# A mixer and mixture-of-experts layer: the first token tile's expert places counted on their own, gathers spread over a pair's first chunks, the down bias moved one pair later

## What is computed

```python
h  = rms_norm(x, g_ffn)                       # x already holds x + mixers(x)
logits = h @ w_router + b_router              # 256 x 32
top_val, top_idx = lax.top_k(logits, 4)
gates = softmax(top_val)
# for each of the 32 experts e, over the tokens that chose it:
hu = h[tok] @ w_up[e] + b_up[e]               # 1024 -> 2048
x_glu, x_lin = split(hu);  x_glu = min(x_glu, 7);  x_lin = clip(x_lin, -7, 7)
act = x_glu * sigmoid(1.702 * x_glu) * (x_lin + 1)
y = (act @ w_down[e] + b_down[e]) * gate      # 1024 -> 1024
x = x + sum of y over the chosen experts
```

## Time and profile before

| | |
|---|---|
| median of 3 runs | 1045.23 us (1041.35 to 1045.49) |
| the profiled execution, its own time | 1047.88 us |
| its span, first to last instruction | 1045.8 us |
| PE busy | 998.6 us (95%), 4512 matmul passes |
| DVE busy, ACT busy | 202.4 us (19%), 114.6 us (11%) |
| DMA, queue of SP | 424.17 MB, 95.5% of 16 engines' span |
| chain that ended last | PE 70%, DMA 28% |
| mean granted TensorE clock | 0.990 |

### The profile page before, as it was taken

One profiled execution on the slowest core, in us unless ns is written; L12 is line 12 of the kernel. 1 busy time (PEld: TensorE's weight loads), 2 busy tenths in 40 slices (PEclk: granted clock), 3 DMA queues, 4 the chain that ended last, 5 costly groups with the idle time before them and its releaser, 6 DMA issues.

```text
span 1045.8 us, 10985 instructions
## 1 busy us (share of the span) xinstructions
PE 998.6 (95%) x4512; PEld 403.1 (39%) x4512; DVE 202.4 (19%) x485; ACT 114.6 (11%) x230; POOL 12.9 (1%) x26
## 2 busy tenths in 40 slices
PE   8999999999999999999999989999898989898997
PEld 4446563434343433333343434342423324242432
DVE  0456132112121111212121211211111211112112
ACT  2426110001010101010100000000001000000000
POOL 0200000000000000000000000000000000000000
PEclk9999989899999999999999999999999999999999
DMA  9955869989999999999999999999999999999996
GB/s 363 402 243 234 361 248 412 417 374 432 430 435 427 437 425 439 425 437 426 436 426 437 431 432 431 431 435 427 436 426 436 429 436 426 436 427 435 427 428 253
DMA packets 22462, 424.91 MB, mean 406 GB/s; under 512 B 3600, under 2 KB 4368, under 8 KB 6704
## 3 DMA queue, kind: packets, MB, share of 16 engines
q1 hardware_dynamic: 22064, 424.17, 95.5%
q10 hardware_dynamic: 384, 0.54, 0.2%
HBM read 423.65 MB, written 1.05 MB: 406 GB/s over the span
## 4 chain that ended last, share of the span: by engine, by line
PE 70%; DMA 28%; another core or an unknown queue 1%; ACT 1%; issue 0%; DVE 0%; SPq 0%
PE psum L1386 30%; DMA everything<-in_w_moe 27%; PE psum L1416 15%; PE psum L1072 4%; PE psum L1281 4%; PE psum L1313 3%; PE psum L1196 3%; PE psum L1039 3%; PE psum L1271 2%; PE psum L1047 2%; PE psum L1064 1%; PE psum L1055 1%; ACT everything L688 1%; PE psum L1322 0%; PE psum L1235 0%
## 5 line engine op out<-in xcount | busy, mean ns | idle before, releaser
L1386 PE MATMUL psum<-everything 128*64 128x512 f32 x2048 | 456.9, 596 | 5.3 <-DMA everything<-in_w_moe 5.1
L1416 PE MATMUL psum<-everything 128*64 128x512 f32 x1024 | 229.7, 601 | 31.8 <-DMA everything<-in_w_moe 24.3
L1386 PEld LDWEIGHTS psum<-everything 128*64 128x64 f32 x2048 | 139.7, 137 | 293.0 <-issue 283.3
L1416 PEld LDWEIGHTS psum<-everything 128*64 128x64 f32 x1024 | 76.1, 138 | 173.6 <-issue 158.3
L1004 DVE TENSOR_SCALAR everything<-psum 128x512 f32<-128x512 f32 x32 | 22.2, 692 | 408.1 <-PE psum L1386 408.1
L721 DVE TENSOR_TENSOR everything<-psum,everything 128x512 f32<-128x512 f32 (+1 forms) x38 | 25.0, 663 | 287.0 <-PE psum L1281 284.1
L1281 PEld LDWEIGHTS psum<-everything 128*128 128x128 f32 x512 | 61.7, 200 | 13.6 <-issue 13.6
L1281 PE MATMUL psum<-everything 128*128 128x128 f32 x512 | 64.7, 286 | 0.0
L679 ACT ACTIVATE everything<-everything 128x512 f32<-128x512 f32 x32 | 20.2, 630 | 380.1 <-DVE everything L1004 380.1
L1313 PE MATMUL psum<-everything 128*128 128x512 f32 x128 | 57.7, 593 | 0.0
L1072 PE MATMUL psum<-everything 128*128 128x512 f32 x96 | 42.1, 594 | 0.0
(11 more groups left out here) (160 smaller groups left out, 299.9 us busy)
## 6 DMA issues: line engine op xcount, KB each, us to landing
everything<-in_w_moe SPq DMA_DIRECT2D x81, 4096.0 KB, 44.6
everything<-in_w_moe SPq DMA_DIRECT2D x25, 2048.0 KB, 17.3
everything<-in_w_moe SPq DMA_DIRECT2D x8, 1024.0 KB, 8.5
everything<-in_w_in SPq DMA_DIRECT2D x3, 2048.0 KB, 26.7
everything<-in_w_out SPq DMA_DIRECT2D x2, 2048.0 KB, 11.7
everything<-in_w_mem_kv SPq DMA_DIRECT2D x1, 2048.0 KB, 17.8
everything<-in_w_moe SPq DMA_DIRECT2D x4, 512.0 KB, 36.0
everything<-in_w_in SPq DMA_DIRECT2D x1, 1024.0 KB, 9.4
```

What stands on the lines that cost most here:

```text
L1386: mm = pe.matmul(psum[r:r + SLOTS, bank], XT[:, k, r:r + SLOTS], weights[i][:, column:column + N], start=k == 0 and not first, stop=k == K ...
L1416: mm = pe.matmul(psum[r:r + SLOTS, DOWN_BANKS[n]], actT[:, 2 * i + k, r:r + SLOTS], slot[:, column:column + N], start=i == 0 and k == 0, s ...
```

## The change

- The placing is done tile by tile. `count(t)` on PE writes tile t's counts beside its router logits, `place_and_select(t)` on DVE makes `spots` and `sel` of that tile. The count of tile 0 stands inside the last part of `mix`, and two router steps of tile 1 ahead of `turn_h2(3)`. `gather_first(0, ...)` gathers tile 0's half of the first four pieces before the count of tile 1, `gather_first(1, ...)` adds tile 1's. All `keep_warm` matmuls are gone. Two of the four up biases of pair 0 move into the pair, to chunk 3.
- In every pair after the first, the gather's first four pieces and one of the four combining matmuls stand ahead of chunk 0, the gather's other four and one combining matmul ahead of chunk 1, and the last two ahead of chunk 2. PE waits for `y_ready` of both halves before chunk 0.
- `turn_act` of the second half stands ahead of the second down chunk rather than the third.
- The down biases are combined in pair 1, two matmuls after its third down chunk and two after its fourth, and are loaded in that pair. The sums in the result banks are begun by `combine` of pair 0.
- In SP's queue the last two chunks of pair 14 are loaded singly (`pair_before_last`).
- ACT's squares go to `XT_cols` as scratch, no longer to `sig` and `sel`.

The diff, cut to what the text speaks of:

```diff
+            def pair_before_last():
+                q = PAIRS - 2
+                for d in range(TWOS - 1):
+                    wait_used(q, 2 * d + 1)
+                    sp.dma_start(two_slots[d], two_chunks(q * TWOS + d)).then_inc(two_in[d], 16)
+                    credit(d)
+                for j, done in ((PAIR_CHUNKS - 2, two_in[TWOS - 1]), (PAIR_CHUNKS - 1, quarters_in[0])):
+                    wait_used(q, j)
+                    sp.dma_start(slots[j], chunk(q * PAIR_CHUNKS + j)).then_inc(done, 16)
+                for arrived in (tenth_half_in, *quarters_in[1:]):
+                    sp.sem_inc(arrived, 16)
...
+            def place_and_select(t):
+                dve.wait_ge(placed, t + 1)
+                step(V.scalar_tensor_tensor(out=spots[:, t], in0=psum[:, ROUTE_BANKS[t], 64:64 + E], scalar=1.0,
+                                            in1=chosen[:, t], op0=ALU.add, op1=ALU.mult))
+                for e in range(2):
+                    last = V.tensor_scalar(sel[:, t, e * SLOTS:(e + 1) * SLOTS], iota_one, spots[:, t, e:e + 1],
+                                           rs_ffn[:, t:t + 1], ALU.is_equal, ALU.mult)
+                last.then_inc((sel_first, sel_ready)[t], 1)
...
             choose(0)
+            place_and_select(0)
             add_mixed(3)
...
-            mix(3, range(5, 8))
-            keep_warm(3, H2_LAST)
+            mix(3, range(5, 7))
+            count(0)
+            mix(3, range(7, 8))
+            route(1, range(2))
             turn_h2(3)
-            route(1)
+            route(1, range(2, KD))
...
+            gather_first(0, range(KD // 2))
+            count(1)
             pe.wait_ge(bup_in, 16 * 4)
             pe.wait_ge(whose_ready, 1)
-            bias(0, (0, 1), start=True)
-            keep_warm(3, H2_LAST)
-            pe.wait_ge(chosen_ready, 2)
-            pe.matmul(psum[:, 5, 64:128], before, chosen.rearrange("p t e -> p (t e)"), start=True, stop=False)
-            pe.matmul(psum[:, 5, 96:128], ones, chosen[:, 0], start=False, stop=True).then_inc(placed, 1)
-            bias(0, (2, 3), start=True).then_inc(biased, 1)
-            keep_warm(4, 7)
-            gather(0, range(KD // 2), FIRST_GATHER_BANKS)
+            bias(0, (0, 2), start=True)
+            gather_first(1, range(KD // 2))
...
-                if not first:
-                    pe.wait_ge(up_read, 2 * q)
-                    gather(q)
-                    if not own:
-                        combine(q - 1)
...
+                    elif not first and j == 0:
+                        pe.wait_ge(up_read, 2 * q)
+                        gather(q, range(KD // 2))
+                        if not own:
+                            combine(q - 1, (0,), start=second)
+                        pe.wait_ge(y_ready, 2 * q)
                         pe.wait_ge(xt_ready, 2 * q + 1)
...
+                    elif j == 1:
+                        gather(q, range(KD // 2, KD))
+                        if not own:
+                            combine(q - 1, (1,), start=second)
+                    elif j == 2:
+                        if not first and not own:
+                            combine(q - 1, (2, 3), start=second)
                         pe.wait_ge(xt_ready, 2 * q + 2)
...
-                    if i == 2:
+                    if i == 1:
                         turn_act(q, 1)
...
-                if first:
-                    combine_bdown()
+                    if second and i >= 2:
+                        combine_bdown((0, 1) if i == 2 else (2, 3))
```

More of the change, by code:

```diff
@@ L484, in _ @@
             second_pair()
-            with sp.Fori(2, PAIRS - 1) as q:
+            with sp.Fori(2, PAIRS - 2) as q:
                 pair(q, q)
+            pair_before_last()
             last_pair()
@@ L674, in _, with pair @@
                                  ).then_inc(gatesT_ready, 1)
-            def pair(q, first=False):
+            def pair(q, bdown=False):
                 for i in range(2):
@@ L683, in pair @@
                                              ).then_inc(back_ready, 1)
-                    elif first:
-                        act.wait_ge(act_ready, 2)
+                    elif bdown:
+                        act.wait_ge(act_ready, 2 * q + 2)
                         act.dma_start(Y[0:E, :], b_down[0]).then_inc(bdown_in, 16)
@@ L698, in pair @@
                     nc.scalar.activation(Y[:, n * N:(n + 1) * N], psum[:, DOWN_BANKS[n]], ACT.Copy).then_inc(y_ready, 1)
-            pair(0, first=True)
-            with act.Fori(1, PAIRS) as q:
+            pair(0)
+            pair(1, bdown=True)
+            with act.Fori(2, PAIRS) as q:
                 pair(q)
@@ L945, in _ @@
             choose(1)
[L948 to L955, removed]
+            place_and_select(1)
             def build_sel(q):
@@ L1218, in turn_h2, with route @@
                 mm.then_inc(h2_turned, 1)
-            def route(t):
-                for k in range(KD):
+            def route(t, steps=range(KD)):
+                for k in steps:
                     if t == 1 and k == 4:
@@ L1228, in route, with count @@
                                    start=k == 0, stop=k == KD - 1)
[L1229 to L1235, removed]
+                if k == KD - 1:
+                    mm.then_inc(routed, 1)
+            def count(t):
+                pe.wait_ge(chosen_ready, t + 1)
+                here = psum[:, ROUTE_BANKS[t], 64:64 + E]
+                mm = pe.matmul(here, before, chosen[:, t], start=True, stop=t == 0)
+                if t == 1:
+                    mm = pe.matmul(here, ones, chosen[:, 0], start=False, stop=True)
+                mm.then_inc(placed, 1)
             pe.wait_ge(ones_ready, 1)
@@ L1342, in wait_chunk, with pair @@
                     pe.wait_ge(arrived, q * 16 + 16 * (TWO_LOADS[j // 2] - 1 if j % 2 == 0 else 0))
-            def pair(q, p, first=False, own=False):
-                if not first:
-                    pe.wait_ge(up_read, 2 * q)
-                    gather(q)
-                    if not own:
-                        combine(q - 1)
+            def pair(q, p, first=False, second=False, own=False):
                 half = UP_CHUNKS // 2
@@ L1354, in pair @@
                         pe.wait_ge(xt_first, 1)
-                    elif j == first:
-                        pe.wait_ge(xt_ready, 2 * q + 1)
-                    elif j == half // 2:
+                    elif not first and j == 0:
[4 more added lines that the diff above has]
+                        pe.wait_ge(y_ready, 2 * q)
+                        pe.wait_ge(xt_ready, 2 * q + 1)
+                    elif first and j == 1:
+                        pe.wait_ge(xt_ready, 1)
+                    elif j == 1:
[5 more added lines that the diff above has]
+                            combine(q - 1, (2, 3), start=second)
                         pe.wait_ge(xt_ready, 2 * q + 2)
-                    if first and j == 1:
-                        gather(0, range(KD // 2, KD), FIRST_GATHER_BANKS)
-                        turn_gates()
-                    if j == half - 1 and not first:
+                    if j == half - 1 and first:
+                        bias(0, (1, 3), start=True).then_inc(biased, 1)
+                    elif j == half - 1:
                         pe.wait_ge(whose_ready, q + 1)
@@ L1394, in pair @@
                             mm.then_inc(half_used, 1)
+                        if first and i == 0 and j == 1:
+                            gather_first(0, range(KD // 2, KD))
+                            gather_first(1, range(KD // 2, KD))
+                            turn_gates()
                     if not last:
@@ L1430, in _ @@
             pair(0, 0, first=True)
+            pair(1, 1, second=True)
             overflow = overflowing(pe)
-            with pe.Fori(1, PAIRS) as q:
+            with pe.Fori(2, PAIRS) as q:
                 pair(q, q)
```

28 lines of the change are left out of this document (19 added, 9 removed).

## The result

The changed kernel takes 1039.2 us (median of 7 runs, 1037.76 to 1039.81), the kernel before 1045.23 (7 runs, 1041.35 to 1048.24). The ratio is 0.9941, with a 95% interval of 0.9923 to 0.9959. So the change is worth 6.0 us where 10.9 were forecast; the time lies in the stated range, towards its upper end, and on the forecast side.

What follows compares the result with a forecast made beforehand. The stream of expert-weight loads, not PE, was taken to bound the kernel. Gains of 4.5 (first gap), 3.8 (second gap), 1.0 (between) and 1.6 (tail) summed to 10.9 us, giving a median of 1034.3 us, range 1030 to 1040.

Steps and rivals of the forecast that it cites:

- The bound: Whole kernel: the stream of loads sets the end, 58.4 us a pair at 431 GB/s against PE's 53.8 us.
- Rival 3: PE is the bound after all, so its own savings count: 24.3 us, to 1021 us; chance 0.05.
- Rival 4: New waits inside the pair make it slower, from 57.0 us of PE a pair on; chance 0.05.
- The two gaps and what lies between: Dry stretches of the stream at 146-152 and 211-217 us close, gaining 4.5 and 3.8 us; between them 1.0 us.
- the last one of the sum: Traced span less 10.9 us is 1034.9; that execution being 2.65 us above the median, the median comes to 1034.3 us.
- rival 1: A half-clock stretch in the last pair, where PE is the chain, costs up to 3.2 us: 1037.5 us; chance 0.12.
- Rival 2: Low clock holds the front back, pair 0 starts past 145 and the first gap stays: 1038.8 to 1042 us; chance 0.10.
- The cover of the first gap: Stream at 146-152 us: the whole 4.9 us loss is regained for any pair 0 start up to about 143.5.
- The front's steps: Before pair 0: router ends 0.5 to 0.7 us sooner, choice at 137.4, pair 0 starts at 140.5, not 146.93.
- the second gap: Stream at 211-217 us, 161 GB/s while waiting for pair 1 to use chunks 0 and 1; closing it gains 3.8 us.
- The tail: Pairs 14 and 15: PE ends at T + 69.5 instead of T + 71.1, a gain of 1.6 us.
- T: Time when chunks 8 and 9 of pair 14 land, 966.4 us in the kernel before.

Runs made afterwards that it cites:

- e3: Changed kernel with part of the matmuls left out in pairs 2 to 15, about 6.9 us of PE a pair, all loads kept; 1038.37 us.
- e4: Changed kernel with four more matmuls of 256 columns, about 1.8 us, in each of pairs 2 to 15; 1040.12 us.
- e9: The kernel before, unchanged, run again for a second profile; that execution took 1045.15 us, median of 8 runs 1045.65 us.
- e2: Changed kernel with the old front: both tiles placed together, ten filler matmuls back, all four up biases ahead of pair 0; 1041.7 us.
- e8: Changed kernel with ten `keep_warm` filler matmuls back at three places in its new front; 1041.4 us.
- e5: Changed kernel with the down bias back at the end of pair 0; 1040.94 us.
- e7: Changed kernel with the last two chunks of pair 14 loaded together again; 1038.79 us.
- e10: Kernel before with the new front and the down bias in pair 1, nothing else of the change; 1040.26 us.
- e1: Kernel before with only the front's part of the change; 1042.63 us.
- e11: Changed kernel without the spread of gather and combining and without the single loads at the end of pair 14; 1038.57 us.

## Why the prediction was right or wrong

**The bound** was right: e3 and e4 move PE's work by some 97 us down and 25 us up for less than 1 us of time. Rival 3 (1021) is out. Rival 4 is out as well: a pair takes PE 53.7 us, well under 57.

**The two gaps and what lies between** were right for the execution that I read. There, the load of chunk 10 is issued at 134.86 and the last load ends at 1033.2, 898.3 us; in the changed kernel they are 136.08 and about 1025.6, 889.5. The last load fades out there instead of stopping at once, so its end is good to half a us:

```profile
1024.00:1025.00 1.00, 1.00 (x8) 0.34 (x6) 0.00 (x0) 0.00 (x0) 0.00 (x0) 1.00 0.74 295
1025.00:1026.00 1.00, 1.00 (x6) 0.29 (x4) 0.00 (x0) 0.00 (x0) 0.00 (x0) 1.00 0.42 172
1026.00:1027.00 1.00, 1.00 (x8) 0.38 (x6) 0.00 (x0) 0.00 (x0) 0.00 (x0) 1.00 0.07 29
```

The stream gained about 8.8 us, where 4.5 + 3.8 + 1.0 = 9.3 were forecast. The span went from 1045.8 to 1037.2, 8.6 us; with the 1.0 us of the late first projection taken off it would be 9.6, against 10.9.

**The step that failed is the last one of the sum**: "its time is 2.65 us above the median of 1045.23, and the median comes to 1034.3". I took the traced execution's gain off the median. But that execution was slow, and what sets it apart from e9, an execution near the median, is mainly that TensorE ran at 1.2 GHz in its front and for longer behind the down bias. These losses made up much of the gaps that the change closes. In e9 the gaps are smaller, and the span to the changed kernel differs by 1043.1 - 1037.2 = 5.9 us, which is what the medians say. I had seen the low clock in the earlier trace rows and priced it for the changed kernel alone, as rivals 1 and 2, not for the kernel before. The gain should have been set against a full-clock front: 2.5 us at pair 0's start, not 6.4. Two profiles of the kernel before carry this account; of its other executions only the times are known.

**The cover of the first gap** was mis-sized: "for any start up to about 143.5". In e2 pair 0 starts at 143.85 and the stream falls to 234 GB/s:

```profile
144.00:146.00 2.00, 2.00 (x10) 0.62 (x10) 0.37 (x3) 0.00 (x0) 0.00 (x0) 1.00 0.99 426
146.00:148.00 2.00, 2.00 (x13) 0.85 (x10) 0.00 (x0) 0.00 (x0) 0.00 (x0) 1.00 0.79 234
```

A load issued to a dry queue does not move bytes at once. In the kernel before, the issue is at 148.90 and full rate is there at about 151.3 (82, 66 and 311 GB/s in the three us from 149 on). In e2 the load is issued at 145.83, some 0.4 us before pair 0's loads end, and 0.9 us of stream are lost from 146 to 148 all the same. The forecast took this start as free.

e8 shows a second cover, which the forecast left out. Its first gap stays closed (427 GB/s from 146 to 152, 408 in the changed kernel). Its stream dips later, when SP issues the load of pair 1's fourth chunk at 161.94 (160.74 in the changed kernel):

```profile
162.00:164.00 2.00, 2.00 (x12) 0.68 (x10) 1.50 (x3) 0.00 (x0) 0.00 (x0) 1.00 1.05 307
164.00:166.00 2.00, 2.00 (x12) 0.61 (x10) 0.00 (x0) 0.00 (x0) 0.00 (x0) 1.00 0.89 373
```

That is 0.8 us. The six half chunks ahead of it are 6.3 MB, 14.6 us at 431 GB/s, so by my estimate they ran out at about 162.1 in e8 and 161.9 in the changed kernel. The fourth load came 0.2 us before that in e8, and 1.2 us before it in the changed kernel, which shows no dip there (438 GB/s from 162 to 164). It is issued 18.4 us after pair 0's first matmul in both, so a later start of pair 0 uses up this margin first. No run tries the fourth load alone.

**The front's steps.** Pair 0 starts at 142.34, 141.3 without the late first projection, where 140.5 was forecast. From the choice to pair 0's start are 3.35 us, all at full clock, where 3.1 were worked out. The choice came at 138.99, or 138.0 with the 1.0 us taken off, 0.6 later than the 137.4 forecast. Nearly all of that is tile 1's router: its rest ends at 137.76 (136.8), 0.2 us sooner than before and not 0.5 to 0.7. The wait for POOL, which was not in the sum, ends at the same time and adds 0.1 at most. The low clock of the earlier trace rows begins at about 138.3 by finer stretches, not at 138.6 as I had it. Rival 2 did not come about. The Trainium skill, page "TensorE: Matmul & The Clock Gate", Part 1, says that activity releases the throttle; by it the fillers should have paid. No profile here shows them doing so. In the steady pairs the traces lean its way: e4, where PE is busiest, has no lower clock, and e3, where it waits longest, has the most. But e2, which waits as the changed kernel does, has none either.

**The down bias** is worth 1.7 us by e5 (2.2 against e7) and 2.4 by e10 against e1, less than the 3.8 of the second gap in the first trace. There the low clock held the gather up by 2.56 us; in e9 and e1 by 1.6, in e5 not at all. So this drop was no oddity of the first profile: it stands in all three profiles in which the whole gather follows the down bias, and only its length varies. One sign failed, that the down bias takes 0.27 us a pass as the up bias does. It takes 0.48 in pair 1 (four passes below) and 0.46 in e5, at full clock; why was not tried.

```profile
239.52 1.98 PE L1353 MATMUL psum<-everything 32*128 32x512 f32 x4
```

So most of the 4.30 us of the earlier trace rows was not the low clock.

**The tail** was forecast at 1.6 us and is 0.7. I put it down to the split and to chunk 0 starting at once. Chunk 0 does start as its load lands, at T + 19.4, yet with neither spread nor split (e11) the tail is 0.6 us shorter still; the gain comes from `turn_act`. In the forecast a pair took PE 53.05 us. It takes 53.7, since I costed the spread at nothing and looked for its price in waits, where it is in the breaks between kinds of matmuls. The drop of the clock that I had as rival 1 came in pair 14 (chunk 8: 5.35 us) and cost nothing: in e5 and e8 chunk 8 runs at full clock (3.65 us) and the tail is 70.3 us as well. The Trainium skill, page "DMA: Bandwidth & Descriptors", section on the anatomy of one DMA, gives a transfer issued from GpSimd a fixed part of about 2 us, most of it between the last byte and the semaphore. These loads are SP's, and the section does not say that such a part stops the stream behind it, so the 2 us that I read into it do not follow. e7 shows no cost of splitting a load at the end of a full queue, and no gain.

**What stays open.** e8 costs 2.2 us of median, and its profile accounts for 1.4 (span 1038.6 against 1037.2), 0.8 of it in the dip at the fourth chunk. Why the first projection takes 15.9 or 16.8 us was not tried.

## What to carry to other kernels

Where a stream of loads is the bound, look for the stretches in which it runs dry and ask what gives back its buffers, for every load behind the gap and not the first alone; work moved on the engine counts only there and behind the last load. Before a gain is carried from a profiled execution to the median, ask what made that execution slower than the median, and whether the change would remove just that. Splitting a run of like matmuls into pieces has a price on PE of its own, about 0.1 us a break here, even where every wait is covered.

## What the runs showed of the hardware

- The clock of one and the same front differs from execution to execution: the old front ran at 0.66 in one and at 1.00 in two others (e2, e9), with PE busy throughout.
- Behind the four down-bias matmuls of pair 0 the clock fell in all three profiles in which the whole gather follows them (before, e9, e1), for 3 to 7 us. It did not in e5, where half a gather follows, nor in the ten others, which have the down bias in pair 1.
- In the steady pairs the low clock was most frequent where PE waits longest (mean 0.96 in e3) and absent where it hardly waits (1.00 in e4). It was absent in e2 too, which waits as the changed kernel does, so waiting alone does not decide it.
- The kernel before spreads over 7 us, the changed one over 2. That the changed one has less work where a drop would let the stream run dry is a likely reason, not a shown one.
- Matmuls of 32 rows by 512 columns took 0.27 us a pass in the up bias and 0.46 to 0.48 in the down bias, both at full clock.
- PE can be 99% busy (780 of 785 us in e4) beside a stream that is the bound.
- A dry DMA queue took about 2.4 us from issue to full rate in the kernel before (148.90 to about 151.3), while queued loads followed each other at 431 GB/s without a seam.
